# A transformer trunk on one core: two projection stages moved into the experts' block

## The reference

```python
for layer in range(2):
    mod = silu(c) @ ada_w[layer] + ada_b[layer]
    sh1, sc1, gt1, sh2, sc2, gt2 = split(mod, 6)
    h = rms_norm(x, g[layer, 0]) * (1 + sc1) + sh1
    y = hybrid_attention(h) @ w_out  if layer == 0 else  rwkv7(h) @ w_o
    x = x + gt1 * y
    h = rms_norm(x, g[layer, 1]) * (1 + sc2) + sh2
    x = x + gt2 * peer(h)        # product-key experts, 16384 of them
```

## Time and profile before

| what | value |
|---|---|
| median of 3 runs | 4395.73 us (4393.61 to 4401.9) |
| span of the profiled execution | 4398.3 us |
| TensorE busy | 4228.2 us, 96% |
| VectorE, ScalarE, GpSimd busy | 54%, 33%, 10% |
| mean granted TensorE clock | 0.979 |

### The profile page before, as it was taken

How to read it: one execution, slowest core, us unless ns; L and a number is a source line. 1 busy time by engine, 2 the same in 40 slices (tenths; PEclk the granted TensorE clock), 3 DMA queues, 4 the chain that set the end, 5 groups by cost and what they waited for, 6 DMA issues and landing times. The chain is left out here.

```text
span 4398.3 us, 60426 instructions
## 1 busy us (share of the span) xinstructions
PE 4228.2 (96%) x22388; PEld 3429.5 (78%) x22388; DVE 2371.8 (54%) x3986; ACT 1446.0 (33%) x1979; POOL 452.0 (10%) x388
## 2 busy tenths in 40 slices
PE   6998999999999999998989999799999999999999
PEld 3454888888888888885779889588888888888887
DVE  6764794555234555556366664489455523444444
ACT  2252333333222222224433433333333322222222
POOL 0001341000000000001422231234100000000000
PEclk9998999999999999998989999899999999999999
DMA  6301245566656666644411110224565565565554
GB/s 265 139 1 68 91 143 168 203 208 208 200 172 241 220 236 225 228 170 166 169 51 47 33 45 25 101 92 142 175 209 204 191 210 178 185 204 182 200 181 139
DMA packets 290730, 694.18 MB, mean 158 GB/s; under 512 B 48360, under 2 KB 116456, under 8 KB 282640
## 3 DMA queue, kind: packets, MB, share of 16 engines
q1 hardware_dynamic: 288272, 675.32, 45.4%
q0 software_dynamic: 2304, 16.78, 1.1%
HBM read 534.72 MB, written 157.32 MB: 157 GB/s over the span
## 5 line engine op out<-in xcount | busy, mean ns | idle before, releaser
L1395 DVE TENSOR_TENSOR pe_lo<-pe_raw,pe_hi 128x2048 fp32r<-128x2048 f32 x222 | 508.9, 2292 | 1267.8 <-ACT pe_hi L1156 1267.8
L825 PE MATMUL bank<-pe_hh,pe_hi 128*128 128x512 f32 x2304 | 913.5, 396 | 36.9 <-DVE pe_lo L1310 32.8
L827 PE MATMUL bank<-pe_hh,pe_lo 128*128 128x512 f32 x2304 | 899.6, 390 | 0.0
L826 PE MATMUL bank<-pe_hl,pe_hi 128*128 128x512 f32 x2304 | 899.4, 390 | 0.0
L826 PE MATMUL bank<-pe_al,pe_hi 128*128 128x512 f32 x2048 | 796.7, 389 | 0.0
L825 PE MATMUL bank<-pe_ah,pe_hi 128*128 128x512 f32 x2048 | 796.7, 389 | 0.0
L827 PE MATMUL bank<-pe_ah,pe_lo 128*128 128x512 f32 x2048 | 796.7, 389 | 0.0
L1156 ACT ACTIVATE pe_hi<-pe_raw 128x2048 fp32r<-128x2048 f32 x270 | 516.6, 1913 | 580.7 <-PE bank L827 580.2
L825 PEld LDWEIGHTS bank<-pe_hh,pe_hi 128*128 128x128 f32 x2304 | 433.7, 188 | 125.4 <-issue 35.8
L827 PEld LDWEIGHTS bank<-pe_hh,pe_lo 128*128 128x128 f32 x2304 | 433.4, 188 | 91.5
L826 PEld LDWEIGHTS bank<-pe_hl,pe_hi 128*128 128x128 f32 x2304 | 434.2, 188 | 85.5
(11 more groups left out here) (321 smaller groups left out, 5042.5 us busy)
## 6 DMA issues: line engine op xcount, KB each, us to landing
pe_raw<-in_stream SPq DMA_DIRECT2D x272, 1024.0 KB, 5.6
acts<-h SPq DMA_DIRECT2D x128, 512.0 KB, 7.1
gates<-pe_shared SPq DMA_DIRECT2D x32, 2048.0 KB, 7.4
pe_w<-gates SPq DMA_DIRECT2D x32, 2048.0 KB, 10.3
h<-acts SPq DMA_DIRECT2D x128, 512.0 KB, 4.1
ada_ring<-in_ada_w SPq DMA_DIRECT2D x32, 768.0 KB, 6.3
at_ada_ring<-in_ada_w POOLq DMA_DIRECT2D x16, 1024.0 KB, 7.3
rwkv_proj<-rp_out SPq DMA_DIRECT2D x64, 256.0 KB, 2.2
```

The lines of the kernel that those rows point to most:

```text
L825: nc.tensor.matmul(out, left[0], right[0], start=start, stop=False)
L826: nc.tensor.matmul(out, left[0], right[1], start=False, stop=False)
L827: return nc.tensor.matmul(out, left[1], right[0], start=False, stop=stop)
L1395: nc.vector.tensor_tensor(lo[:, side], raw[:, side], hi[:, side].bitcast(F32), ALU.subtract).then_inc(low, 1)
```

## The change

Attention's last block and the RWKV residual block are no longer blocks of their own. `stage_attention` and `project_residual` return their lists as a `Front`, and `stage_peer` runs each list at the head of its own one. The block boundary and `end_stage` between them are gone. With it:

- The first two weight pairs are loaded by `load_first`: in layer 0 at the head of SyncE's list, in layer 1 behind the last load of `w_o`. ScalarE makes both `hi` in one piece each between the squares (`split_first`), GpSimd makes both `lo`. The piecewise split of pair 0 (lines 1186, 1187, 1265, 1310) is removed.
- In layer 0 the first `sum_modulation` takes only the 8 gate columns; the other 24 are summed behind `mean_of_squares`. VectorE finishes them behind `invert_root`, and SyncE holds back the load of `keys` until they are summed.
- In layer 1 the tiles of the residual block lie behind the space of `raw`, `hi` and `lo`.

```diff
+    def sync(sp, load_first):
+        load_first()
+        for m in range(WR, DC):
+            sp.wait_ge(wo_done, m - WR + 1)
+            sp.dma_start(wt[:, m % WR], io["w_out"][m]).then_inc(wo_loaded[m % WR], 16)
+        sp.wait_ge(ada_rest_summed, 1)
...
+        for c in range(DC):
+            if 1 <= c <= 2:
+                split_first(c - 1)
+            act.wait_ge(added, c + 1)
+            square_rows(K, act, norm, c, K.hc)
+        root_of_mean(K, act, norm, 7, 0)
...
+        invert_root(K, dve, norm, 0)
+        finish_modulation(K, dve, 0, ada_rest_summed, mod_rest_done, bank=6, first=EARLY // P + GATE_COLS,
+                          n=48 - EARLY // P - GATE_COLS, subs=(1,))
+        dve.wait_ge(mod_rest_done, 2)
...
+        sum_modulation(K, ada_acc, ada_summed, bank=6, first=EARLY // P, n=GATE_COLS)
...
+        mean_of_squares(K, pe, norm, 7, K.hc)
+        sum_modulation(K, ada_acc[:, GATE_COLS * P:], ada_rest_summed, bank=6, first=EARLY // P + GATE_COLS,
+                       n=48 - EARLY // P - GATE_COLS)
...
-                load(0, 0, wait=False)
+                def load_first():
+                    for n in range(2):
+                        load(n, n, wait=False)
+
+                front.sync(sp, load_first)
                 sp.dma_start(keys[:, :, :].rearrange("p a b -> p (a b)"), io["subkeys"][layer]).then_inc(keys_loaded, 16)
-                load(1, 1, wait=False)
-                sp.wait_ge(first_low, 1)
                 for n in range(FIRST_UP + 2):
                     load(n + 2, n % 2)
...
-                            if k == 0:
-                                pe.wait_ge((first_low, low)[r], 1)
+                            if k == 0 and r == 0:
+                                pe.wait_ge(low, 1)
...
+                front.tensor(pe)
                 first_up()
...
+                front.scalar(act, lambda n: make_high(n, n))
                 for c in range(DC):
                     act.wait_ge(scaled, c + 1)
                     nc.scalar.activation(hh[:, c, :], K.hc(c), ACT.Identity, bias=shift_of(K, layer, 1, c)).then_inc(h_high, 1)
-                    if c == 2:
-                        act.wait_ge(raw_loaded[0], loads(0, 0))
-                        nc.scalar.activation(hi[:, 0, 0], raw[:, 0, 0], ACT.Copy).then_inc(first_high, 1)
-                        nc.scalar.activation(hi[:, 0, 1], raw[:, 0, 1], ACT.Copy).then_inc(high, 1)
...
-                gp.wait_ge(high, 1)
-                nc.gpsimd.tensor_tensor(lo[:, 0, 1], raw[:, 0, 1], hi[:, 0, 1].bitcast(F32), ALU.subtract).then_inc(low, 1)
-                for n in range(1, FIRST_UP):
+                if front.gpsimd is not None:
+                    front.gpsimd(gp)
+                for n in range(FIRST_UP):
                     make_low(n, n % 2)
...
-                    if c == 4:
-                        dve.wait_ge(first_high, 1)
-                        nc.vector.tensor_tensor(lo[:, 0, 0], raw[:, 0, 0], hi[:, 0, 0].bitcast(F32),
-                                                ALU.subtract).then_inc(first_low, 1)
...
+            else:
+                sp.wait_ge(loaded, 16 * (m - RESIDUAL_EARLY + 1))
+        load_first()
+        sp.wait_ge(projected, DC)
...
+        for c in range(DC):
+            if c + 2 < DC:
+                weights_high(c + 2)
+            else:
+                split_first(c + 2 - DC)
+            act.wait_ge(added, c + 1)
+            square_rows(K, act, norm, c, square)
+        root_of_mean(K, act, norm, 7, 6)
...
-            stage_attention(K, wt, w_loaded)
-            K.end_stage()
+            attention_out = stage_attention(K, wt, w_loaded)
...
-            stage_peer(K, 0, shared)
+            stage_peer(K, 0, shared, attention_out)
             K.end_stage()
-            stage_rwkv(K, across, shared)
-        K.end_stage()
+            residual = stage_rwkv(K, across, shared)
```

More of the change, by code:

```diff
@@ L8 @@
+from collections import namedtuple
 from contextlib import ExitStack
@@ L199 @@
 LATE_TILE = 2 * D
+GATE_COLS = 8
 def stage_modulation(K, wt, w_loaded):
@@ L728, in stage_attention @@
         norm = NormSems(K, "n01")
[L729 to L798, removed]
@@ new lines, in tensor, with mean_of, project @@
+    def tensor(pe):
+        def mean_of(a):
+            pe.wait_ge(sub_squared, a + 1)
+            if a >= 2:
+                pe.wait_ge(sub_std, a - 1)
+            nc.tensor.matmul(K.ps[a % 2][:, :], K.const("ones_v"), sq[:, a % 2, :], start=True,
+                             stop=True).then_inc(sub_meaned, 1)
+        def project(m, first, end):
+            for k in range(first, end):
+                if m == 0 and k < 4:
+                    pe.wait_ge(sub_normed, k + 1)
+                last = nc.tensor.matmul(K.ps[2 + m % 4][:, :], wt[:, m % WR, k, :], heads[:, k, :],
+                                        start=(k == 4), stop=(k == 3))
+            return last
+        sum_modulation(K, ada_acc, ada_summed, bank=6, first=EARLY // P, n=GATE_COLS)
+        for m in range(WR):
+            mean_of(m)
+            pe.wait_ge(wo_loaded[m], 16)
+            project(m, 4, DC)
+        for m in range(DC):
+            if m >= WR:
+                pe.wait_ge(wo_loaded[m % WR], 32)
+                pe.wait_ge(added, m - 3)
+                project(m, 4, DC)
+            project(m, 0, 4).then_inc(wo_done, 1)
+        mean_of_squares(K, pe, norm, 7, K.hc)
+        sum_modulation(K, ada_acc[:, GATE_COLS * P:], ada_rest_summed, bank=6, first=EARLY // P + GATE_COLS,
+                       n=48 - EARLY // P - GATE_COLS)
@@ L801 @@
+    return Front(sync, scalar, vector, tensor, None)
 GATE_SCALE = 4096.0
@@ new lines, in project_residual, with raw @@
+    square = lambda c: sq[:, c, :]
+    loaded = K.sem("rw_loaded")
+    w_high = K.sem("rw_w_high")
+    w_low = K.sem("rw_w_low")
+    y_high = K.sem("rw_y_high")
+    y_low = K.sem("rw_y_low")
+    projected = K.sem("rw_projected")
+    added = K.sem("rw_added")
+    norm = NormSems(K, "n11")
+    x_loaded = K.sem("rw_x_loaded")
+    def raw(m):
+        if m < RESIDUAL_EARLY:
+            return early[:, 2 * m:2 * m + 2, :].rearrange("p a (k m) -> p (a k) m", m=P)
+        return wt[:, m - RESIDUAL_EARLY]
@@ new lines, in sync, with gpsimd @@
+    def sync(sp, load_first):
+        for m in range(RESIDUAL_EARLY, DC):
+            sp.dma_start(wt[:, m - RESIDUAL_EARLY], K.io["w_o"][m]).then_inc(loaded, 16)
+            if m == RESIDUAL_EARLY:
+                sp.wait_ge(loaded, 16)
+                sp.dma_start(K.x[:, :, :], K.io["x_parked"]).then_inc(x_loaded, 16)
+            else:
+                sp.wait_ge(loaded, 16 * (m - RESIDUAL_EARLY + 1))
+        load_first()
+        sp.wait_ge(projected, DC)
+    def gpsimd(gp):
+        for m in range(1, DC):
+            gp.wait_ge(w_high, m + 1)
+            nc.gpsimd.tensor_tensor(wl[:, m % 2], raw(m), wh[:, m % 2].bitcast(F32), ALU.subtract).then_inc(w_low, 1)
@@ new lines, in vector @@
+    def vector(dve):
+        dve.wait_ge(w_high, 1)
+        nc.vector.tensor_tensor(wl[:, 0], raw(0), wh[:, 0].bitcast(F32), ALU.subtract).then_inc(w_low, 1)
+        for c in range(DC):
+            dve.wait_ge(y_high, c + 1)
+            nc.vector.tensor_tensor(yl[:, c, :], K.hc(c), yh[:, c, :].bitcast(F32), ALU.subtract).then_inc(y_low, 1)
+        dve.wait_ge(x_loaded, 16)
+        for m in range(DC):
+            dve.wait_ge(projected, m + 1)
+            nc.vector.scalar_tensor_tensor(out=K.x[:, m, :], in0=K.ps[m % 4][:, :],
+                                           scalar=K.mod[:, layer, 16 + m:17 + m], in1=K.x[:, m, :],
+                                           op0=ALU.mult, op1=ALU.add).then_inc(added, 1)
+            gather_squares(K, dve, norm, m - 1, square)
+        invert_root(K, dve, norm, 6)
+        dve.wait_ge(norm.inverted, 1)
@@ new lines, in scalar, with weights_high @@
+    def scalar(act, split_first):
+        def weights_high(m):
+            if m < RESIDUAL_EARLY:
+                act.wait_ge(early_loaded, 16 * RESIDUAL_EARLY)
+            else:
+                act.wait_ge(loaded, 16 * (m - RESIDUAL_EARLY + 1))
+            if m >= 2:
+                act.wait_ge(projected, m - 1)
+            nc.scalar.activation(wh[:, m % 2], raw(m), ACT.Copy).then_inc(w_high, 1)
+        weights_high(0)
+        for c in range(DC):
+            nc.scalar.activation(yh[:, c, :], K.hc(c), ACT.Copy).then_inc(y_high, 1)
+            if c == 1:
+                weights_high(1)
+        for c in range(DC):
+            if c + 2 < DC:
+                weights_high(c + 2)
+            else:
+                split_first(c + 2 - DC)
+            act.wait_ge(added, c + 1)
+            square_rows(K, act, norm, c, square)
+        root_of_mean(K, act, norm, 7, 6)
@@ new lines, in tensor @@
+    def tensor(pe):
+        for m in range(DC):
+            pe.wait_ge(w_low, m + 1)
+            if m >= 4:
+                pe.wait_ge(added, m - 3)
+            for k in range(DC):
+                if m == 0:
```

(5 more changed lines are left out.)

122 lines of the change are left out of this document (38 added, 84 removed).

## The result

| | median | runs | ratio to the kernel before |
|---|---|---|---|
| kernel before | 4401.64 us | 4393.61 to 4411.22, 10 runs | |
| changed kernel | 4380.82 us | 4377.22 to 4397.73, 10 runs | 0.9956, interval 0.9947 to 0.9964 |

By the ratio the change makes the kernel 0.44% faster, 19 us (16 to 23 by the interval); the two medians differ by 20.8 us. The forecast was 25.5 us less, a ratio of 0.9942, which lies outside this interval. The direction is right. The time of 4380.82 us lies inside the stated range of 4361 to 4382 us by little more than 1 us, and outside the likeliest case's own range of 4361 to 4378 us. The profiled execution of the changed kernel has a span of 4379.2 us, 19.1 less than that of the kernel before.

A forecast was written before the change was run, and what follows sets the result against it. TensorE, without idle time in the expert stages, was taken as the bound, leaving only the two exchanges to gain. Layer 0's -17.4 and layer 1's -8.1 sum to -25.5 us; 4395.7 - 25.5 = 4370.2 us, range 4361 to 4382.

The forecast's parts named there:

- likeliest case: The whole change working as forecast, 4370.2 us, with its own range of 4361 to 4378 us; chance 0.67.
- Bound: Both expert stages keep TensorE busy throughout their 1544 us; only the two exchanges count, and their gain reaches the program's end.
- 24 columns leave the head: Layer 0, head of attention's last block: 16 records instead of 64 precede the first mean; -10.5 us.
- They come back behind the mean: Layer 0: 48 records behind the mean delay the first scaled chunk; +1.9 us, bounds +0.2 and +4.2.
- Pair 0: Experts' opening: weights split early, first matmul 2.3 us behind the first scaled chunk; -8.8 us layer 0, -8.7 layer 1.
- The clock in pair 0: Experts' first pair: half clock expected again in both layers; 0 in the sum, 1 us either way per layer.
- Boundary: Layer 1, between residual projection and experts: the removed block boundary saves as much as layer 0's; -1.2 us.
- The gather: Layer 1, last gather of squares: held by GpSimd's second `lo`; +1.8 us, bounds 0 and +2.7 (addition into x held too).
- Rival 1: Experts' openings: a GpSimd `lo` still holds VectorE's two-input operations, 9 us over both layers, 4379 us; chance 0.11.
- rival 3: Pair 0's first matmul still waits for late loads or `hi`; gain only about 8 us, 4388 us; chance 0.07.
- rival 4: Experts' loops run slower under a new program layout; 0.83% longer pitch eats all 25.5 us; chance 0.05.
- Rival 2: Layer 0: moved columns cost what they saved, through half clock under the sums and at the projection; 4378 us; chance 0.10.

The follow-up runs named there:

- late_split: Changed kernel with the old loads and piecewise split of pair 0, keeping merged blocks and moved columns; ratio to the kernel before 0.9979.
- place_yh: Changed kernel with 8 more words in front of w_o's tile, so split activations and weights both stand 8 off modulo 512; profiled once, span 4382.2 us.
- low_after_gather: Changed kernel, but in layer 1 GpSimd makes pair 1's low half only after the last gather of squares; profiled once, span 4370.9 us.
- columns_at_head2: Changed kernel with all 32 modulation columns summed at the head of attention's last block again; ratio to the kernel before 0.9964.
- pad_wh: Changed kernel with 8 more words in front of the residual block's split weights, later tiles unmoved; profiled once, span 4379.6 us.
- layer0_only: Changed kernel with layer 1 as in the kernel before: own residual block, old tile places, piecewise split; ratio to the kernel before 0.9961.
- three_edits: Changed kernel with eight gate columns summed separately, layer 1's pair 1 `lo` behind the last gather, and `wh` moved to 4096 words; ratio to the kernel before 0.9948.

## What of the prediction held, and the steps that failed

**Bound.** Right: the expert stages take the same 1544 us, and what the exchanges gain arrives at the end.

**24 columns leave the head, -10.5.** The root moved from 75.8 and 77.5 us behind the head to 65.6 (seven profiles) or 67.2 (two): 8.6 to 11.9, by where the clock falls. Right.

**They come back behind the mean, +1.9.** From root to scaled chunk 5.3 us before. With the 24 columns moved: 5.9, 6.0, 6.0 and 6.1 us, and 8.1, 8.2 and 8.4 us in three others, so +0.7 to +3.2. late_split, with the same sums, has 6.2. The new wait is the one forecast, but its size is two values and not one: it depends on whether the clock falls early under the sums. The changed kernel's own three profiles all had the cheap one, which is luck: the same layer 0 had the dear one in three of four other profiles.

**Pair 0, -8.8 and -8.7.** From scaled chunk to first matmul 11.1 and 11.0 us became 2.3 and 2.3. late_split shows that the early loads and splits carry it, not the merge. The clock in pair 0 scattered as allowed: from its first matmul to the copy 11.9 to 13.2 us in layer 0 and 12.1 to 13.4 us in layer 1, in kernels of both kinds.

**Boundary, -1.2.** From root to scaled chunk in layer 1 5.42 us became 4.09: -1.3. Right.

**The gather, +1.8.** The gather itself cost +1.45: the mechanism was right, the size a little less, because GpSimd's second `lo` ran 2.2 us beyond the start of the addition into x, not 2.5. The mechanism behind the upper bound of +2.7 is excluded: the addition, with one operand in PSUM, ran its 0.75 us beside the `lo`. This agrees with the Trainium skill, "SBUF — State Buffer", "Who interferes with whom", in both halves of its rule. The prediction left out what the longer wait can do to the mean behind it: from the last addition to the root the way grew by 1.45, 1.45 and 2.0 us in the changed kernel's three profiles, and by 3.4 in place_yh, where the mean ran at half clock.

**The step that failed in the sum: a term that was missing.** The tiles of layer 1's residual block moved, and the prediction gave this move no price at all. It cost seven chunks of 0.16 us, +1.1 us, in TensorE's own pace; late_split and low_after_gather, where the gather isn't held, have the root 1.1 and 1.6 us later than the kernel before. The 0.6 us more at the program's end are a second term without a price.

**The step that failed in the time: what the sum was taken off.** The prediction wrote that its terms are taken off the median, 4395.7 - 25.5 = 4370.2, and took the 8 us between three runs as their scatter. Over ten runs the median of the same kernel is 4401.64 us and they span 17.6 us; in three other comparisons it is 4400.06 to 4404.21. So of the 10.6 us by which 4370.2 was too low, 5.9 are the starting point, and 4.7 are the gain (20.8 between the medians for 25.5).

**The sum.** Per exchange: forecast -17.4 and -8.1; the changed kernel's three profiles against the two of the kernel before show 85.9 against 105.6, -19.6, and 74.5 against 82.0, -7.5. With the other four profiles of the same layer 0 its mean is 87.8, -17.8. With layer 1's -7.5 and the 0.6 us more at the end that makes -24.7, and the three ratios have a mean of 24 us, so a forecast of 25.5 us was off by 1 to 2 us, about the two terms that were missing. That it agrees so well is luck in part: terms too dear and too cheap cancel. The first comparison showed only 19 to 21 us, the second 27; what made the first one smaller was mostly not a step of the prediction but scatter of the stages around the exchanges, 8 us in where the head stands for one and the same program (320.3, 324.3, 328.3).

**The rivals.** Rival 1 is excluded: `hl` and not a `lo` releases pair 0. So are rival 3, by the openings of pair 0, and rival 4, by the expert stages. Rival 2 is excluded as a whole by columns_at_head2; its first part, half clock under the sums, came true in part in three profiles.

**Open.** Why weights and activations at different places make a matmul 7 ns longer isn't shown, nor which modulus is the true one: 16 words are excluded by pad_wh and more than 128 aren't needed, so 32, 64 and 128 are left. The 0.6 us at the program's end were not looked into. Why the way between the exchanges scatters (2325 to 2336 us in the twelve profiles) wasn't tried.

## What to carry to other kernels

When a stage in which TensorE is never idle stands behind another, look at the chain between the last matmul of the one and the first of the other, and let everything in it that depends only on weights be done before: the opening was worth 8.7 us each time. The 48 records of one column took 0.11 us each at full clock and 0.2 at half; behind a mean they fill a wait, but the clock may fall under them (after 2.7 us in layer0_only), so give the consumer only those that it needs first. When tiles are moved to make room, compare the matmul durations of the untouched loop before and after. And take a forecast off a median of many runs: three runs here stood 6 us below ten.

## What the runs showed of the hardware

- A float32r matmul of 128x512 lasts 389 ns when the weight tile and the moving tile begin at the same place modulo 512 words in their partitions (both 8 in before and place_yh; both 0 in three_edits), and 396 or 398 ns in the median when they begin 8 or 16 words apart (after, pad_wh); for 24 matmuls 5.44 against 5.60 us. Slices of the weight tile 128 words apart are equally fast, so 128 is the largest modulus that these runs allow.
- A gather of two SBUF inputs beside GpSimd's subtraction took 2.13 to 2.29 us instead of 0.68 and ended half a microsecond behind it; an addition with one input in PSUM beside the same subtraction kept its 0.75 us.
- One and the same program of 4381 us differs by 20 us between ten runs of one comparison (4377.2 to 4397.7 us). The granted clock fell from 1.00 to 0.50 some 2.7 us into the single-column sums in layer0_only and 5.0 us into them in after.
